# A LayerNorm-GLU encoder block on eight cores: first four token tiles transposed in fp32, their scale and bias applied out of PSUM, transfers re-priced in the planner

## The reference, cut to what matters

```python
x = layer_norm(x, ln_in_g, ln_in_b)                  # 2048 x 1024 per core
u = x @ w_in                                         # -> q, k, v, conv-GLU, gates
y_a = windowed_gqa(q, k, v, rel_bias, sink) @ w_attn_out
glu = u_conv[..., :512] * sigmoid(u_conv[..., 512:])
y_c = silu(layer_norm(depthwise_conv31(glu) + conv_b)) @ w_conv_out
mix = (sigmoid(g_a) * y_a + sigmoid(g_c) * y_c) @ w_out
h = layer_norm(alpha * x + mix)
out = layer_norm(alpha * h + (silu(h @ w_gate) * (h @ w_up)) @ w_down)
```

## Time and profile before

| what | value |
|---|---|
| median of 3 runs | 907.42 us (906.82 to 907.58) |
| the profiled execution's own time | 908.76 us |
| its span on the slowest core (core 3) | 907.2 us |
| the other cores' spans | 902.6 to 906.6 us |
| PE busy | 860.9 us (95%) |
| DVE, ACT, POOL busy | 500.2, 252.6, 203.5 us |

### The profile page before, as it was taken

One profiled execution on the slowest core, in us unless ns is written; L12 is line 12 of the kernel. 1 busy time (PEld: TensorE's weight loads), 2 busy tenths in 40 slices (PEclk: granted clock), 3 DMA queues, 4 the chain that ended last, 5 costly groups with the idle time before them and its releaser, 6 DMA issues.

```text
span 907.2 us, 14222 instructions; the slowest of 8 cores (902.6 to 907.2 us)
## 1 busy us (share of the span) xinstructions
PE 860.9 (95%) x4788; PEld 412.4 (45%) x4788; DVE 500.2 (55%) x787; ACT 252.6 (28%) x389; POOL 203.5 (22%) x291
## 2 busy tenths in 40 slices
PE   3899999899999999999999999999999999999993
PEld 1345557534444444444444444444444444444441
DVE  5899366587878886697772212145551212123644
ACT  1233355753636352433332111100011111110000
POOL 4245003132040321532233321111121111100211
PEclk9999999999999999999999999999999999999998
DMA  9696658384332413638789998432345545501221
GB/s 208 167 181 117 150 133 151 59 178 150 124 109 76 141 64 117 164 137 208 189 208 222 162 167 124 71 70 106 124 121 82 80 70 77 84 3 47 94 93 47
DMA packets 47897, 110.56 MB, mean 122 GB/s; under 512 B 12913, under 2 KB 13041, under 8 KB 47441
## 3 DMA queue, kind: packets, MB, share of 16 engines
q0 software_dynamic: 21600, 41.72, 30.9%
q1 hardware_dynamic: 26226, 67.93, 22.7%
HBM read 124.09 MB, written 27.26 MB: 167 GB/s over the span
## 4 chain that ended last, share of the span: by engine, by line
PE 85%; DMA 5%; DVE 4%; issue 3%; ACT 1%; POOL 1%; SPq 0%; DVEq 0%; ACTq 0%; POOLq 0%
PE ps L929 32%; PE ps L561 20%; PE ps L953 17%; PE ps L890 4%; PE ps L858 3%; PE ps L849 3%; DMA h_rows<-xr 2%; PE ps L756 1%; DMA xr<-x_rows 1%; PE ps L677 1%; DMA lnrow<-lnp 1%; PE ps L789 1%; PE ps L511 1%; PE ps L528 1%; PE ps L626 1%
## 5 line engine op out<-in xcount | busy, mean ns | idle before, releaser
L937 DVE TENSOR_TENSOR hid<-ps,sgb 128x512 bf16<-128x512 f32 x88 | 60.8, 691 | 215.0 <-PE ps L929 212.1
L929 PE MATMUL ps<-hT,wEa 128*128 128x512 bf16 x704 | 154.6, 379 | 0.9 <-DMA xr<-x_rows 0.9
L929 PE MATMUL ps<-hT,wEb 128*128 128x512 bf16 x704 | 154.7, 379 | 0.0
L953 PE MATMUL ps<-wdn,hid 128*128 128x512 bf16 x704 | 152.3, 379 | 0.0
L935 ACT ACTIVATE sgb<-ps 128x512 f32<-128x512 f32 x88 | 52.6, 597 | 313.9 <-PE ps L929 313.1
L561 PE MATMUL ps<-x0T,wga 128*128 128x512 bf16 x512 | 118.5, 379 | 1.8 <-POOL mT L870 1.0
L953 PEld LDWEIGHTS ps<-wdn,hid 128*128 128x128 bf16 x704 | 68.9, 98 | 83.0
L929 PEld LDWEIGHTS ps<-hT,wEa 128*128 128x128 bf16 x704 | 68.7, 98 | 83.2 <-issue 1.4
L929 PEld LDWEIGHTS ps<-hT,wEb 128*128 128x128 bf16 x704 | 68.6, 98 | 81.9
L870 POOL TENSOR_TENSOR mT<-gab,gab 128x512 bf16<-128x512 f32 x32 | 48.8, 1537 | 123.2 <-DVE gab L864 78.7
L561 PEld LDWEIGHTS ps<-x0T,wga 128*128 128x128 bf16 x512 | 49.1, 98 | 60.3 <-issue 4.0
(11 more groups left out here) (102 smaller groups left out, 930.5 us busy)
## 6 DMA issues: line engine op xcount, KB each, us to landing
xa<-x SPq DMA_DIRECT2D x16, 512.0 KB, 8.3
xb<-x SPq DMA_DIRECT2D x16, 512.0 KB, 4.3
x_rows<-xb SPq DMA_DIRECT2D x16, 512.0 KB, 2.6
xr<-x_rows SPq DMA_DIRECT2D x16, 512.0 KB, 5.4
h_rows<-xr SPq DMA_DIRECT2D x16, 512.0 KB, 6.2
hr<-h_rows SPq DMA_DIRECT2D x16, 512.0 KB, 3.3
out<-hr SPq DMA_DIRECT2D x16, 512.0 KB, 2.6
wEa<-wg POOLq DMA_DIRECT2D x22, 256.0 KB, 4.7
```

The lines of the kernel that those rows point to most:

```text
L929: ins = e.matmul(bank(B), w[:, kc, :], hTv[tc][:, kc, :], start=(kc == 0), stop=(kc == 7))
L937: sc.add("dve", C_DVE, lambda e, U=U, sg=sg, c2=c2: e.tensor_tensor(hid[ffc][:, c2 * 512:(c2 + 1) * 512], bank(U), sg[:, :], ALU.mult), re ...
L953: ins = e.matmul(bank(B), hid[k][:, c0:c0 + 128], wdn[k][:, half * 512:(half + 1) * 512], start=(k == 0), stop=(k == NFF - 1))
```

## The change

The change has four parts. Tiles 0 to 3 no longer pass through `ln_in`: in `ln_first` DVE normalizes a tile in one pass (mean and `rsX`, no scale, no bias), PE transposes it in fp32, and the scale and bias, which after the transpose differ by partition and not by column, are applied while the blocks leave PSUM: four blocks by ACT, four by DVE. `small` carries the scale and bias as 16 more columns. The four L528 products stay, since tiles 4 to 15 still use `lnin`, but get a later priority (L544 now). The loads are recorded in another order and with other dependencies: `small` and the fp32 identity come between the first tiles, the weights `wgl` wait for tile 1 and then for each tile's `rsX`, and the loads of tiles 4 to 7 wait until a weight `wgl` has landed. And the planner's numbers change: `SWITCH` 2.6 to 1.3, `DMA_RATE` 0.19 to 0.31, the cost of a `cast_load` doubled, other costs for `poly`; the 16 Silu operations of the convolution are one run that no other table may interrupt, during which one PSUM bank is kept free for transposes.

```diff
-    SWITCH = 2.6
+    SWITCH = 1.3
-    DMA_RATE = 0.19
+    DMA_RATE = 0.31
...
+                    if running and op.table is not None and not op.run:
+                        continue
...
-                        if len(bank_free) < len(need) or used.get(b.cls, 0) + len(need) > self.caps[b.cls]:
+                        if len(bank_free) < len(need) + (running and b.cls != "tr") or used.get(b.cls, 0) + len(need) > self.caps[b.cls]:
...
-        sc.dma("pool", kb, lambda e: e.dma_start(out=dst_ap, in_=src_ap), reads=reads, writes=writes)
+        sc.dma("pool", 2 * kb, lambda e: e.dma_start(out=dst_ap, in_=src_ap), reads=reads, writes=writes)
...
-    for t in range(4):
+    load(512, xa[0][:, :], x_d[0:128, :], ["xa0", ("xl", 0)])
+    load(28, small[:, :], small_d, ["small"])
+    load(512, xa[1][:, :], x_d[128:256, :], ["xa1", ("xl", 1)])
+    load(64, ident32[:, :], ident_d, ["ident32"])
+    for t in range(2, 4):
         load(512, xa[t][:, :], x_d[t * 128:(t + 1) * 128, :], ["xa%d" % t, ("xl", t)])
...
+    def ln_first(t):
+        xs, xn = xa[t], "xa%d" % t
+        stats(xs, xn, mvX[:, 2 * t:2 * t + 2], ("mvX", t))
+        inv_std(rsX[:, t:t + 1], mvX[:, 2 * t + 1:2 * t + 2], EPS, 1, [("mvX", t)], [("rsX", t)])
+        sc.add("dve", 0.8, lambda e: e.tensor_scalar(
+            xs[:, :], xs[:, :], mvX[:, 2 * t:2 * t + 1], rsX[:, t:t + 1], ALU.subtract, ALU.mult),
+            reads=[xn, ("mvX", t), ("rsX", t)], writes=[xn])
+        for h in range(2):
+            B = Bank("tr")
...
+                    ins = e.transpose(bank(B)[:, i * 128:(i + 1) * 128], xs[:, kc * 128:(kc + 1) * 128],
+                                      ident32[:, :])
...
+                if h == 0:
+                    sc.add("act", 0.35, lambda e, i=i, B=B, dst=dst, g_ap=g_ap, b_ap=b_ap: e.activation(
+                        dst, bank(B)[:, i * 128:(i + 1) * 128], AF.Identity, bias=b_ap, scale=g_ap),
+                        reads=[B, "small"], writes=[("x0T0", t)])
+                else:
+                    sc.add("dve", 0.25, lambda e, i=i, B=B, dst=dst, g_ap=g_ap, b_ap=b_ap: e.tensor_scalar(
+                        dst, bank(B)[:, i * 128:(i + 1) * 128], g_ap, b_ap, ALU.mult, ALU.add),
+                        reads=[B, "small"], writes=[("x0T0", t, 1)])
...
     def ln_in(t):
-        if t >= 4:
-            load(512, xs[:, :], x_d[t * 128:(t + 1) * 128, :], [xn, ("xl", t)])
+        load(512, xs[:, :], x_d[t * 128:(t + 1) * 128, :], [xn, ("xl", t)],
+             reads=["wgl%d" % (t - 4)] if t < 8 else [])
...
+                cast_load(256, wgl[k][:, :], win_d[6 + k], ["wgl%d" % k], reads=[("rsX", i - 1) if i else ("xl", 1)])
...
-        cast_load(256, wqk[k][:, :], win_d[k], ["wqk%d" % k], reads=[("xl", 6 + k)])
+        cast_load(256, wqk[k][:, :], win_d[k], ["wqk%d" % k], reads=[("xl", 5 + k // 3)])
...
-                reads=[B, "small"], writes=[("ycin", cc)], table="silu")
+                reads=[B, "small"], writes=[("ycin", cc)], table="silu").run = True
```

More of the change, by code:

```diff
@@ L41 @@
     __slots__ = ("eng", "fn", "dma", "deps", "preds", "succ", "npred", "sig", "token", "extra",
-                 "cost", "prio", "seq", "table", "banks", "fin", "ready")
+                 "cost", "prio", "seq", "table", "banks", "fin", "ready", "run")
     def __init__(self, eng, fn, dma, cost, prio, seq, table):
@@ L58, in __init__ @@
         self.table = table
+        self.run = False
         self.banks = ()
@@ L161, in arrange @@
         left = len(self.all)
+        runs = sum(1 for op in self.all if op.run)
+        running = False
         while left:
@@ L171, in arrange @@
                             st = max(st, h[-self.NSLOT])
-                    if op.table is not None and op.table != table:
+                    if op.table is not None and op.table != table and not op.run:
                         st_key = st + self.SWITCH
@@ L192, in arrange @@
             ready[e].remove(op)
+            if op.run:
+                runs -= 1
+                running = runs > 0
             for b in op.banks:
@@ L525, in build @@
     sc.add("dve", 0.1, lambda e: e.memset(onesr[0:1, :], 1.0), writes=["onesr"])
[L526 to L531, removed]
@@ L532, in build, with spread_row @@
-    cast_load(32, ident[:, :], ident_d, ["ident"])
-    load(20, small[:, :], small_d, ["small"])
+    def spread_row():
+        for k in range(4):
+            B = Bank("proj")
+            sc.add("pe", 1.8, lambda e, k=k, B=B: e.matmul(
+                bank(B), onesr[0:1, :], lnrow[0:1, k * 512:(k + 1) * 512], start=True, stop=True),
+                reads=["onesr", "lnrow"], writes=[B])
+            sc.add("act", C_ACT, lambda e, k=k, B=B: e.copy(lnin[:, k * 512:(k + 1) * 512], bank(B)),
+                   reads=[B], writes=[("lnin", k // 2)])
@@ new lines, in ln_first, with f_tr @@
+    def ln_first(t):
[7 more added lines that the diff above has]
+            B = Bank("tr")
+            def f_tr(e, h=h, B=B):
+                ins = None
+                for i in range(4):
+                    kc = 4 * h + i
+                    ins = e.transpose(bank(B)[:, i * 128:(i + 1) * 128], xs[:, kc * 128:(kc + 1) * 128],
+                                      ident32[:, :])
+                return ins
+            sc.add("pe", 4 * 0.24, f_tr, reads=[xn, "ident32"], writes=[B])
+            for i in range(4):
+                kc = 4 * h + i
+                dst = x0Tv[0][:, kc, t * 128:(t + 1) * 128]
+                g_ap = small[:, C_LNG + kc:C_LNG + kc + 1]
+                b_ap = small[:, C_LNB + kc:C_LNB + kc + 1]
+                if h == 0:
[6 more added lines that the diff above has]
+                        reads=[B, "small"], writes=[("x0T0", t, 1)])
@@ L552, in xregs @@
     def xregs(tc):
-        return [("x0T%d" % tc, i) for i in range(4)]
+        return [("x0T%d" % tc, i) for i in range(4)] + ([("x0T0", i, 1) for i in range(4)] if tc == 0 else [])
     def proj(wt, wname, tc, B, also=()):
@@ L581, in build @@
         for i in range(4):
[L582 to L585, removed]
+            if tc:
+                ln_in(4 * tc + i)
+                continue
+            for k in (4 + i, i):
+                cast_load(256, wgl[k][:, :], win_d[6 + k], ["wgl%d" % k], reads=[("rsX", i - 1) if i else ("xl", 1)])
+            ln_first(i)
+        if tc == 0:
+            cast_load(32, ident[:, :], ident_d, ["ident"])
+            sc.prio = 104
+            spread_row()
         sc.prio = 105 + 10 * tc
```

9 lines of the change are left out of this document (6 added, 3 removed).

## The result

The changed kernel takes **913.50 us** (before 907.42): the ratio is 1.0067, with a 95% interval of 1.0053 to 1.0081. It is slower, and past the 911.5 at which the predicted range ended.

What follows compares the result with a forecast made beforehand. PE, busy 95% of the span, was taken as the bound, behind a 29.89 us head. Terms +2.4 - 1.3 + 0 - 1.0 = +0.1 on 908.76 gave 908.9, or 907.5 us on the median's scale; range 902.8 to 911.5.

Steps and rivals of the forecast that it cites:

- PE begins with L544, row and tiles through at 26.8: Head: PE still starts when lnrow lands, taken as 12.0 us, and finishes row products and fp32 transposes at 26.8.
- The new wait: Head: PE waits for tile 4 before the first GLU projection, whose start moves from 29.89 to 32.3 us: +2.4 us.
- The old wait: First GLU block: PE's 1.33 us wait for tile 7 at 54.22 us goes: -1.3 us.
- The clock: First GLU products: they start at 1.2 GHz again after PE idles from 26.8 to 31.3 us: 0 (to -2.5).
- The rival of a fast clock: Head: fp32 transposes bring PE to 2.4 GHz, first 64 products take 13.98 us: -2.4, 905.0 us; chance 0.17.
- the row at 170 to 172 us: Profile row before: PE did only fp32 transposes at clock 0.50 at 170 us; at 172 the clock was 1.00.
- The Silu run: Convolution: two gate projections instead of one between the transposes, less PE idling there and behind: together -1.0 us.
- one gate's cover more: Silu run: a second gate projection puts 1.73 us of PE work in the run; 0.2 us gained within it.
- The rest: Everything else: same instructions in slightly different order on a PE busy throughout: 0.
- The sum: Whole kernel: +2.4 - 1.3 + 0 - 1.0 = +0.1 us on the profiled execution's 908.76.
- The head: Start through the first GLU block: a cost of 1.1 us was forecast.
- The rival that ended slower, tile 4 late: Head: tile 4 lands at 32.5 us, GLU starts at 40: +7.7 us, 915 us; chance 0.20.

Runs made afterwards that it cites:

- r1: The change with the four planner prices of before put back, fp32 tiles and Silu rule kept; 908.1 us, 1.0003 to the kernel before.
- r2: The kernel before, head and all (bf16 tiles, old transfer order), with the four new planner prices and the Silu rule; 913.85 us, 1.0066.
- r3: The change without the rule for the Silu run, fp32 tiles and new prices kept; 921.35 us, 1.0143 to the kernel before.
- r10: r2 with the planner's prices of before from the last Silu of the convolution on; 907.9 us, 0.9995 to the kernel before.
- r12: The change with the planner's prices of before from the last Silu on, its head and convolution kept; 909.6 us, 1.0016.
- r15: The kernel before with the Silu rule added, and the new planner prices from the last Silu on; 912.93 us, 1.0061.
- r5: The change with the planner's size of the mix stage's row loads and stores raised from 512 to 1400 KB; 927.5 us, 1.0212.
- r11: r1 with the third and fourth wout loads held until the second tile's rows are stored; two executions, 907.67 and 908.38 us, no ratio.
- r13: The change with the first four FFN weight loads (wEa) moved behind eight more instructions of POOL's list; 918.13 us, 1.0118.
- r16: r10 with the first four FFN weight loads moved behind four more instructions of POOL's list; 906.6 us, 0.9985 to the kernel before.

## Why the prediction was wrong

- **PE begins with L544, row and tiles through at 26.8.** Right in kind: 13.14 and 28.18. `lnrow` came 1.1 us later than I had taken.
- **The new wait.** Right, step by step: `wgl0` landed at 18.2 (17), tile 4 was issued at 18.2 and took 8.3 us (8.4), `x0b` was there at 33.0 (31.3). Mis-sized was the eviction: I took 0.3 us for 128x128 on DVE, and it took 0.41, the upper bound (16 evictions below). The normalizing pass was cheaper than its row, 0.81 for 1.08.

```profile
L579 DVE TENSOR_SCALAR x0T<-ps,small 128x128 bf16<-128x128 f32 x16 | 6.2, 406 | 1.6 <-PE ps L565 1.2
L555 DVE TENSOR_SCALAR xa<-xa,mvX,rsX 128x1024 f32<-128x1024 f32 x4 | 3.1, 806 | 0.0
```

- **The old wait** for tile 7 is gone, as forecast.
- **The clock.** Right: the first 64 products took 16.03 us, not 13.98 (granted clock 0.50 in 34 to 36 us), and the fp32 transposes ran at 0.22 us each to the end. The rival of a fast clock falls for the head. That the full clock doesn't engage for transposes is also what the Trainium skill has (TensorE: Matmul & The Clock Gate, Part 4: PE-mode transpose), against the row at 170 to 172 us. No run here tells whether the transposes or the 5 us of waiting behind them kept the clock low; in r1, with 2.2 us of waiting, the first 64 products still took 15.86 us (core 6).
- **The Silu run.** Right sign, a third of the size: -3.1 instead of -1.0. The working, one gate's cover more, is not shown to be the reason: with the old head (r2) or without the rule (r3, 7.4 to 8.6 us idle) the stretch gained nothing over the 6.9 to 8.4 of before. It takes the rule and the fp32 head together, so the sign was partly luck.
- **The rest: "Everything else is the same instructions in a slightly different order, on a PE that is busy throughout: 0."** This is the step that failed. The order was different by 28 products at a place where PE depends on a store and a load of rows, and it was these products that had kept PE busy there. The change's own diff named the cause, a DMA rate that makes row transfers cheaper in the planner, and I priced the transfers it moved in the head only. Measured, the term is +6.9 us of idle time between 250 and 450 us. r10, r12 and r15 put what the new prices behind the last Silu cost at 4.6 to 6.4 us. With the old prices from there on the change takes 909.6 (r12), inside the predicted range.
- **The sum.** The head +1.7 for +1.1, the Silu run -3.1 for -1.0, the rest +6.9 for 0: together the 5.5 us by which PE's list ends later, where +0.1 was forecast.
- The rival that ended slower, tile 4 late, named a place that was nearly as forecast; the kernel got slower through another.

## What to carry to other kernels

A planner's price is part of the program: when it changes, read the new order wherever an engine waits for a transfer, not only where the code was edited, and count the work that stands between the request and the use. Price a transfer by what it takes in its own stretch (16 us for a store and a reload among weight loads, where the planner had 7); but when you change one price, read the whole order again: in r5 a higher one cured the 3.7 us wait, and the kernel got 13 us slower. When only the slowest of several cores counts, look at a late core's waits: the early one's profile shows none of this.

## What the runs showed of the hardware

A 512 KB row store takes 2.6 to 3.0 us alone and 6 to 10 when it is issued among weight loads on the other queue: `x_rows` among four loads of `wout` (9.8 in r1) or two (6.0 and 7.7 in r11), `h_rows` among four of `wEa` (8.4 in the change, 10.0 before) and, in r13, of `wEa` and of `wEb` (8.7 and 8.9). I had seen the same for the x tiles and not looked for it later.

In every pair of neighbouring cores of the change one is late, by 4.45 us in the median; with the old order and the weights moved out of the way of the stores (r16) the distance is 0.95. The Trainium skill (HBM Reference, Specifications (TRN2)) says that the two cores of a pair share the bandwidth of their memory. That this is why one of them is late is not shown: no run had one core alone.

A wait of PE can cost twice. Behind the 3.61 us of r13 the granted clock fell; its windows on core 3:

```profile
418.00:421.00 3.00, 0.00 (x0) 1.00 0.52 202
421.20:424.60 3.40, 3.40 (x15) 0.50 0.28 112
424.60:427.00 2.40, 2.40 (x18) 1.00 1.03 312
```

So 1.2 GHz for 3.4 us. Behind the 4.54 us of r5 it stood at 0.50 as well, and the next sixteen mix products took 4.58 us instead of 3.62. Behind the 3.73 us at 388 in the change it did not fall.
